# First attention, softmax pipeline: the order of scores and transposes on TensorE

## The reference, cut to what matters

```python
# x, block i of 128 queries: local keys within a window of 128, and all context keys
s_loc = where(valid, q_i @ k_x.T, -1e30);  s_ctx = q_i @ k_c.T
p = softmax(concat([s_loc, s_ctx, sink]));  out = p_loc @ v_x + p_ctx @ v_c
# context queries: context keys only
p = softmax(concat([q_c @ k_c.T, sink]));   out = p @ v_c
```

## Time and profile before

| | us |
|---|---|
| median of 3 runs | 1977.81 (1974.31 to 1981.27) |
| the profiled execution's own time | 1977.15 |
| its span, first to last instruction | 1975.4 |
| busy in the span: TensorE, VectorE, ScalarE | 1661.9, 1138.1, 855.2 |
| mean granted clock of TensorE | 0.915 |
| 126 to 334 us: wait of TensorE's L962 for VectorE's L1932 | 54.7 |

### The profile page before, as it was taken

How to read it: one execution, slowest core, us unless ns; L and a number is a source line. 1 busy time by engine, 2 the same in 40 slices (tenths; PEclk the granted TensorE clock), 3 DMA queues, 4 the chain that set the end, 5 groups by cost and what they waited for, 6 DMA issues and landing times.

```text
span 1975.4 us, 23995 instructions
## 1 busy us (share of the span) xinstructions
PE 1661.9 (84%) x8586; PEld 1327.3 (67%) x8586; DVE 1138.1 (58%) x1780; ACT 855.2 (43%) x1286; POOL 16.8 (1%) x34
## 2 busy tenths in 40 slices
PE   3977777679999996888567999678787798998988
PEld 1853334568888885777456999566565686877768
DVE  2334444354444445678876666565546467777866
ACT  3223333442222333477554554424323265655653
POOL 1000000000000000000001000000000000000000
PEclk8988898879999998899787999778888699999999
DMA  8275552213323332132242666322211078878784
GB/s 304 70 295 175 193 212 85 65 33 96 106 87 104 96 96 64 43 97 85 74 128 88 189 187 184 111 71 83 78 55 41 29 239 274 283 259 272 264 287 160
DMA packets 201823, 279.57 MB, mean 142 GB/s; under 512 B 12314, under 2 KB 111116, under 8 KB 195596
## 3 DMA queue, kind: packets, MB, share of 16 engines
q1 hardware_dynamic: 200064, 269.90, 42.5%
q0 software_dynamic: 1152, 8.39, 1.1%
q10 hardware_dynamic: 524, 0.19, 0.0%
HBM read 277.40 MB, written 1.05 MB: 141 GB/s over the span
## 4 chain that ended last, share of the span: by engine, by line
PE 60%; DVE 21%; DMA 10%; ACT 6%; issue 3%; ACTq 0%; SPq 0%; DVEq 0%; POOL 0%; POOLq 0%
PE bank L390 47%; DMA stage<-in_w_dram 8%; DVE weights_lo L363 4%; PE bank L518 3%; ACT weights_hi L351 2%; PE bank L962 2%; DVE softmax_cols L1912 2%; DVE work L1932 1%; PE bank L946 1%; PE bank L1262 1%; PE bank L563 1%; DMA work<-in_c_ctx_dram 1%; DVE work L596 1%; DVE x_and_ctx L599 1%; PE bank L1312 1%
## 5 line engine op out<-in xcount | busy, mean ns | idle before, releaser
L363 DVE TENSOR_TENSOR weights_lo<-stage,weights_hi 128x1024 fp32r<-128x1024 f32 x428 | 515.8, 1222 | 158.7 <-ACT weights_hi L351 149.9
L351 ACT ACTIVATE weights_hi<-stage 128x1024 fp32r<-128x1024 f32 x428 | 442.4, 1056 | 231.6 <-DMA stage<-in_w_dram 120.6
L390 PE MATMUL bank<-act_hi,weights_hi 128*128 128x256 f32 (+1 forms) x976 | 317.4, 325 | 20.2 <-DVE x_and_ctx L2011 12.8
L390 PE MATMUL bank<-act_lo,weights_hi 128*128 128x256 f32 (+1 forms) x976 | 316.0, 324 | 0.0
L390 PE MATMUL bank<-act_hi,weights_lo 128*128 128x256 f32 (+1 forms) x976 | 315.6, 323 | 0.0
L390 PE MATMUL bank<-weights_hi,ff_hi 128*128 128x512 f32 x560 | 220.3, 393 | 11.5 <-DVE weights_lo L363 9.4
L390 PE MATMUL bank<-weights_hi,act_hi 128*128 128x512 f32 (+1 forms) x488 | 202.9, 416 | 31.7 <-DVE weights_lo L363 15.8
L390 PE MATMUL bank<-weights_hi,ff_lo 128*128 128x512 f32 x560 | 218.2, 390 | 0.0
L390 PE MATMUL bank<-weights_lo,ff_hi 128*128 128x512 f32 x560 | 218.1, 390 | 0.0
L390 PEld LDWEIGHTS bank<-act_hi,weights_hi 128*128 128x128 f32 x976 | 189.8, 194 | 36.0 <-issue 22.1
L390 PEld LDWEIGHTS bank<-act_lo,weights_hi 128*128 128x128 f32 x976 | 189.9, 195 | 13.6
(11 more groups left out here) (338 smaller groups left out, 1957.2 us busy)
## 6 DMA issues: line engine op xcount, KB each, us to landing
stage<-in_w_dram SPq DMA_DIRECT2D x192, 512.0 KB, 4.8
stage<-in_mlp_w_dram SPq DMA_DIRECT2D x128, 512.0 KB, 4.1
ada_rows_in<-in_ada_w_dram SPq DMA_DIRECT2D x40, 1024.0 KB, 5.1
stage<-in_w_in_dram SPq DMA_DIRECT2D x32, 512.0 KB, 4.0
stage<-in_lru_w_in_dram SPq DMA_DIRECT2D x20, 512.0 KB, 3.9
ada_rows_in<-in_ada_w_dram POOLq DMA_DIRECT2D x8, 1024.0 KB, 13.5
stage<-in_attn_w_qkv_dram SPq DMA_DIRECT2D x12, 512.0 KB, 5.0
stage<-in_lru_w_out_dram SPq DMA_DIRECT2D x10, 512.0 KB, 4.7
```

Of the source, the lines that this page charges most:

```text
L351: act.eng.activation(whi[u % NRING][:], stage[u % NSTAGE][:], ACT.Copy).then_inc(sem("hi_ready"), 1)
L363: dve.eng.tensor_tensor(wlo[u % NRING][:], stage[u % NSTAGE][:], whi[u % NRING][:].bitcast(F32), ALU.subtract).then_inc(sem("lo_ready"), 1)
L390: m = pe.eng.matmul(ps, l, r, start=start and j == 0, stop=stop and j == 2, skip_group_check=True)
```

## The change

The scores of half 0 are made ahead of TensorE's loop, and pass h makes those of half h+1, where it made those of half h. Nothing is changed on the other engines, and no instruction is added or taken away: `scores(h + 1)` now stands before the values product of pair (h-3)/2, before `turn_probs(h-1)` and before the ada steps of pass h.

```diff
@@ -980,9 +980,10 @@
                                          skip_group_check=True)
                 m.then_inc(*pe.fill(("O", b)))
 
+            scores(0)
             for h in range(34):
-                if h < 32:
-                    scores(h)
+                if h < 31:
+                    scores(h + 1)
                 if h - 1 in ADA_TURN:
                     ada_cols_pe(pe, ADA_TURN[h - 1], 7)
                 if h >= 3 and h % 2:
```

## The result

The changed kernel takes 1917.38 us (median of 4 runs, 1910.77 to 1922.05), the kernel before 1978.88 us (4 runs, 1974.31 to 1981.27): a ratio of 0.9689, 95% interval 0.9651 to 0.9728, or 61.5 us less by the medians.

What follows compares the result with a forecast made beforehand. The bound was taken to be TensorE's transposes waiting for VectorE's division, queued behind the next maximum, which waits for scores. Savings of 35.3 and 21.6 us sum to 56.9: 1977.15 - 57 = 1920 us, range 1911 to 1938.

Steps and rivals of the forecast that it cites:

- The bank's wait at no cost: Scores wait for banks the exponentials free: costed at nothing, with 1.9 us of room per 512-key pass, some 1.6 per 256-key.
- T0 to T15: From the first transposes of the probabilities to those of pass 15: 73.7 us against 109.02, 35.3 us saved.
- T15 to T30: From the transposes of pass 15 to those of pass 30: 56.2 us against 77.79, 21.6 us saved.
- Two wide halves: Two loop passes with 512 keys: 9.12 us, against 12.6 at full clock in the old order.
- two narrow ones: Two loop passes with 256 keys: 6.34 us.
- The wait at the ada columns: After passes 5 and 11, transposes wait while VectorE takes up the columns and then divides: 1.6 us for those two steps.
- The tail: The stretch from the transposes of pass 30 to the output projection, without scores: left as it is, no saving counted.
- The clock: TensorE taken at 2.4 GHz throughout the stage: 16 us of the saving, with some 41 us from the order.
- the clock goes on falling as now: Rival: TensorE's clock keeps its old share of low clock, 16 us given back, 1936 us; chance 0.15, shared with twice the stalls.
- The transposes' wait: Sign of being right: TensorE's idle time before VectorE's division falls from 54.7 to about 20 us.
- The slower one: Rival: TensorE's clock stays at 1.2 GHz and sets the pace, stage 9.6 us longer, 1986 us; chance 0.03.
- The pages: Rival: ada page loads limited to 180 GB/s bind, the stage ends 15 us earlier, not 57, 1962 us; chance 0.03.

Runs made afterwards that it cites:

- the kernel with the wide part alone: The changed kernel with scores made ahead only in the 16 passes with 512 keys, the later ones making their own as before; 1941.92 us, ratio 0.9831.
- the fitted fillers: The kernel before, old order, with unread products on TensorE where it waited for the division, their number cut to fit the waits; 1958.04 us, ratio 0.9907.
- the last kernel: The changed kernel with VectorE's copies a pass later, ada columns behind the division, and weight splits spread over passes 22 to 25; 1893.79 us, ratio 0.9585.

## Why the prediction was right, point by point

**What bounds it.** Right: the transposes' wait for VectorE's division was the loop's gap, and it went when the scores were ready ahead.

**The bank's wait at no cost.** Right: no wait of TensorE ends at an exponential, not even when the exponentials were doubled. That shows at least 1.36 of the 1.9 us of room and 0.94 of the 1.6.

**The terms.** T0 to T15: forecast 73.7, measured 74.38. T15 to T30: 56.2 and 56.21. Two wide halves 9.12 and, from 168.13 to 177.15 with a single page in each, 9.02; two narrow ones 6.34 and, from 224.94 to 231.21, 6.27. The wait at the ada columns 1.6 and 1.53; from the transposes of half 27 to those of half 28 it was to be 6.7 and was 6.73. The tail was left as it is and gave 0.9. The sum of 56.9 for the stage stands against 57.1, of which 0.9 is that tail. That the sum comes so close is in part luck. In the wide part two errors of opposite sign meet: the plain pairs are 0.1 us shorter each than counted, and the two halves behind the first ada columns took 10.56 us (157.57 to 168.13) where the clock had fallen, 1.5 more than a pair at full clock. With a clock such as the kernel with the wide part alone had, the same term would have measured about 78.4.

**The clock.** Forecast 16 us of the sum, measured 16.3 by the fitted fillers; the order 41 and 39.9. The count of the old order at full clock holds part by part too: 98.2 and 72.2 forecast, 97.59 and 72.88 measured. "2.4 GHz throughout" was a little too much: behind the columns of half 5 it fell, and stood at 0.78 from 160 to 164 us, and it fell again behind the wait of half 28.

```profile
156.00:160.00 4.00, 2.47 (x17) 1.08 (x16) 3.71 (x14) 1.72 (x4) 0.00 (x0) 0.80 0.89 377
160.00:164.00 4.00, 4.00 (x40) 2.23 (x38) 0.30 (x1) 0.90 (x5) 0.00 (x0) 0.78 0.55 174
...
256.00:260.00 4.00, 3.37 (x16) 1.08 (x16) 3.17 (x12) 2.31 (x10) 0.00 (x0) 0.67 0.54 171
```

That part of the rival "the clock goes on falling as now" is real, and in the run with the wide part alone it cost 4 us.

**What was mis-sized.** The transposes' wait was to fall to "about 20 us" and fell to 13.9: the number did not follow from my own terms (seven wide pairs at 0.5, seven narrow ones at 0.8, two turns at 1.6 and the split at 3.5 make 15.8 at most, and 17.1 with the 1.27 us of the tail). The stretches before and behind the stage were to be unchanged, and in the profiled pair they were 9.3 us shorter. Of this, 7.5 lie behind the stage, and the ten profiled executions spread as far there with either order, so no effect of the change shows in them. The medians differ by 61.5 us, 4.6 more than forecast, which is less than either kernel's runs are apart; against the later runs of the kernel before (1974.15 and 1975.86 us) the changed kernel's median is 56.8 and 58.5 us less.

**The rivals.** The slower one, a clock that stays at 1.2 GHz, did not come: granted 0.98 and 0.97. Its price of 1986 was also too low, because it let the values product alone keep its duration. The narrow one takes 1.09 us at full clock and, in the kernel before, took 1.97 in a stretch with a granted clock of 0.50 (the second row; the first is a group of eight transposes at the same clock):

```profile
140.57 1.97 PE L962 MATMUL bank<-ident,work 128*128 128x128 f32 x8 [2.96 <-DVE work L1932]
...
328.05 1.97 PE L978 MATMUL bank<-work 128*64 128x128 f32 x16 [0.78 <-ACT work L1538]
```

That is 0.9 us more for each of seven narrow pairs; no row shows the wide product at the low clock. The Trainium skill's rule for this rival (TensorE: Matmul & The Clock Gate, Part 4: PE-mode transpose), that the full clock does not engage for transposes, is not borne out in this mix: the last kernel holds 1.00 over 66.65 us, of which the transposes, one group in every half, take 16.3, and eight transposes take 1.03 us at a granted clock of 1.00 (178.41 to 179.44) and 1.90 at 0.50 (140.57 to 142.47, ahead of the page of the earlier trace rows). What a long stretch of transposes alone would get, no run here shows. The pages did not bind, at 299 GB/s in the end.

## What to carry to other kernels

When several engines pass a chain of small steps to each other in order, write down for each engine which wait ends last, and count a whole period with the durations of the timeline: the engine that looks slow may only stand behind a step that another could have made a pass earlier. After such a reordering look at once for the next step that waits for something late while ready work stands behind it; here, the place of the copies, of the columns and of a weight split was worth 18.1 us once the scores were ready ahead (139.7 to 121.6 in the stage); what it would be worth in the old order was not run. And gaps on TensorE can cost twice, once as idle time and once by the clock behind them, as those of 1.5 us and more did here.

## What the runs showed of the hardware that was not expected

- An fp32 product with 128 rows, 128 outputs and 512 columns took 0.88 us at full clock, the four of an ada page with 32 outputs each 1.00 us together, and the two of a scores step with 64 rows each 1.06 us together. I had taken the first for 0.53 us.
- Work that nobody needs made the program 17.8 us faster (1958.04 against 1975.86), with TensorE's clock granted at 1.00 where it had been 0.87 and 0.89.
- The clock fell behind waits of about 1.5 us at the ada columns, and not in every execution alike: 0.98 and 0.93 in the mean over the same order. So a profile's saving can be off by some 4 us (74.38 and 78.40) for this stage alone. Waits of 0.5 to 0.75 us, one per pair, left it at 1.00.
